# First weight slices split and summed by quarters, input loaded in four pieces, constants on ScalarE's queue, loads in order of use

## The reference

```
mod = silu(c) @ ada_w + ada_b;  shift, scale, gate = split(mod, 3)
h = rmsnorm(x, g_pre) * (1 + scale) + shift
z = h @ w_in
gates = sigmoid(h @ w_merge + b_merge)
...
out = rmsnorm((g_a * ya + g_b * yb) @ w_out, g_post)
y = x + gate * out
```

## Time and profile before

| what | us |
|---|---|
| median of 3 runs | 933.63 (932.96 to 933.76) |
| profiled execution, its own time | 933.39 |
| span of that execution | 931.6 |
| TensorE matmul busy | 905.5 (97%) |
| VectorE busy | 556.0 (60%) |
| ScalarE busy | 418.0 (45%) |
| GpSimd busy | 54.9 (6%) |
| DMA | mean 252 GB/s, 419 to 421 GB/s in the first 116 us |

### The profile page before, as it was taken

The page is one execution under the profiler, slowest core; times in us unless marked ns, Lnnn a source line. Parts: engine busy times, 40 slices in busy tenths (PEclk is TensorE's granted clock), DMA queues, the critical chain, the costliest instruction groups (busy, mean ns, idle before and its releaser), DMA issues.

```text
span 931.6 us, 18640 instructions
## 1 busy us (share of the span) xinstructions
PE 905.5 (97%) x7762; PEld 868.6 (93%) x7762; DVE 556.0 (60%) x808; ACT 418.0 (45%) x514; POOL 54.9 (6%) x38
## 2 busy tenths in 40 slices
PE   3899999999999999999999999999999999999997
PEld 1788989999999999999999999999999999999997
DVE  4777776476675767757576655336454444445554
ACT  4323227455565565646554434444344333343330
POOL 0000000001101010110102122000000000000000
PEclk9899999999999999999999999999999999999999
DMA  9999975848585684857675565476687666645535
GB/s 373 418 421 419 419 311 171 332 158 284 183 323 197 226 301 158 314 179 293 231 268 187 199 203 183 154 271 189 254 323 281 257 243 255 246 161 181 182 136 186
DMA packets 43322, 234.57 MB, mean 252 GB/s; under 512 B 9088, under 2 KB 14592, under 8 KB 16256
## 3 DMA queue, kind: packets, MB, share of 16 engines
q1 hardware_dynamic: 43264, 233.72, 68.0%
HBM read 219.33 MB, written 14.38 MB: 251 GB/s over the span
## 4 chain that ended last, share of the span: by engine, by line
PE 94%; DVE 2%; DMA 2%; issue 1%; POOL 1%; ACT 0%; SPq 0%; DVEq 0%; POOLq 0%; ACTq 0%
PE bank L429 25%; PE bank L430 24%; PE bank L431 24%; PE bank L481 4%; PE bank L482 3%; PE bank L483 3%; PE bank L403 3%; PE bank L413 1%; DMA raw<-stream 1%; PE bank L577 1%; PE bank L622 1%; PE bank L561 1%; DMA sel<-sel_in 1%; DVE raw L1429 1%; DVE w_lo L1028 0%
## 5 line engine op out<-in xcount | busy, mean ns | idle before, releaser
L429 PE MATMUL bank<-h_hi,w_hi 128*128 128x264 f32 x1280 | 368.2, 288 | 2.2 <-DVE w_lo L1028 1.3
L430 PE MATMUL bank<-h_lo,w_hi 128*128 128x264 f32 x1280 | 362.9, 283 | 0.0
L431 PE MATMUL bank<-h_hi,w_lo 128*128 128x264 f32 x1280 | 362.5, 283 | 0.0
L1028 DVE TENSOR_TENSOR w_lo<-raw,w_hi 128x2048 fp32r<-128x2048 f32 x119 | 272.3, 2288 | 142.1 <-PE bank L431 142.0
L712 ACT ACTIVATE w_hi<-raw 128x2048 fp32r<-128x2048 f32 x120 | 229.7, 1914 | 44.0 <-DMA raw<-stream 23.8
L429 PEld LDWEIGHTS bank<-h_hi,w_hi 128*128 128x128 f32 x1280 | 241.1, 188 | 8.5 <-issue 6.4
L430 PEld LDWEIGHTS bank<-h_lo,w_hi 128*128 128x128 f32 x1280 | 241.3, 189 | 0.3
L431 PEld LDWEIGHTS bank<-h_hi,w_lo 128*128 128x128 f32 x1280 | 240.1, 188 | 0.0
L481 PE MATMUL bank<-h_hi,w_hi 128*128 128x264 f32 x256 | 76.1, 297 | 4.5 <-DVE h_lo L1110 4.5
L482 PE MATMUL bank<-h_lo,w_hi 128*128 128x264 f32 x256 | 73.7, 288 | 0.0
L483 PE MATMUL bank<-h_hi,w_lo 128*128 128x264 f32 x256 | 73.6, 288 | 0.0
(11 more groups left out here) (180 smaller groups left out, 1181.4 us busy)
## 6 DMA issues: line engine op xcount, KB each, us to landing
raw<-stream SPq DMA_DIRECT2D x120, 1024.0 KB, 5.0
ada_ring<-ada SPq DMA_DIRECT2D x32, 1024.0 KB, 15.5
raw<-first_w SPq DMA_DIRECT2D x16, 1024.0 KB, 13.1
gate_ring<-ada SPq DMA_DIRECT2D x16, 1024.0 KB, 6.6
s_t<-sret SPq DMA_DIRECT2D x8, 1024.0 KB, 5.0
v_all<-v_dram SPq DMA_DIRECT2D x8, 1024.0 KB, 7.4
nret_s<-s_t SPq DMA_DIRECT2D x8, 1024.0 KB, 8.1
x_t<-xT SPq DMA_DIRECT2D x1, 2112.0 KB, 7.7
```

What stands on the lines that cost most here:

```text
L429: pe.matmul(out, wh[:, cols], hi[:, k, :], start=(k == 0), stop=False)
L430: pe.matmul(out, wh[:, cols], lo[:, k, :], start=False, stop=False)
L431: mm = pe.matmul(out, wl[:, cols], hi[:, k, :], start=False, stop=(k == depth - 1))
L1028: dve.tensor_tensor(lo, raw[:, c % 3, :], hi.bitcast(f32), ALU.subtract).then_inc(lo_ready, 1)
```

## The change

The core of the diff:

```
+BY_QUARTER, HIGH_BY_QUARTER = 5, 2
...
-            sp.dma_start(x_t[:, :, :], xT).then_inc(x_in, 16)
-            sp.dma_start(c_in[:, :, :], cT).then_inc(const_in, 16)
...
-            for p in range(8):
-                if p == 0:
-                    load_ada(p, range(4))
-                    load_slice(0)
-                else:
-                    load_ada(p, (0, 1))
-                    load_slice(2 * p)
-                    load_ada(p, (2, 3))
-                load_slice(2 * p + 1)
+            for n in range(4):
+                sp.dma_start(x_t[:, 4 * n:4 * n + 4, :], xT[:, 4 * n:4 * n + 4, :]).then_inc(x_in[n], 16)
+            load_ada(0, range(4))
+            load_slice(0)
+            for p in range(1, 8):
+                load_ada(p, (0, 1))
+                load_slice(2 * p - 1)
+                load_ada(p, (2, 3))
+                load_slice(2 * p)
+            load_slice(15)
...
-                if q - 1 in COND_VISITS:
-                    v = COND_VISITS.index(q - 1) + 1
-                    if v < 8:
-                        load_cond(v)
+                for s in range(2):
+                    if q - 1 - s in COND_VISITS[:7]:
+                        load_cond(COND_VISITS.index(q - 1 - s) + 1, s)
...
-                    if u == 2:
+                    if u == 1:
                         pe.wait_ge(x_sum, KT // 2)
...
+            def quarter(j, n):
+                if n == 0:
+                    pe.wait_ge(h_lo_ready, j // 2 + 1)
+                if n < 3:
+                    pe.wait_ge(lo_quarter, 3 * j + n + 1)
+                else:
+                    pe.wait_ge(lo_ready, j + 1)
+                for u in (2 * n, 2 * n + 1):
+                    if u < OWN_IN[j % 2]:
+                        own(j, u)
+                    else:
+                        pass_through(j, u - OWN_IN[j % 2])
...
             ada_phase(0)
             select(0)
+            for n in range(4):
+                quarter(0, n)
+            ada_phase(1, (0, 1))
+            quarter(1, 0)
+            ada_phase(1, (2, 3))
+            quarter(1, 1)
+            select(1)
+            quarter(1, 2)
+            quarter(1, 3)
+            for p in range(1, 7):
+                if 2 * p < BY_QUARTER:
+                    for n in range(4):
+                        quarter(2 * p, n)
+                else:
+                    even_slice(2 * p)
                 ada_phase(p + 1)
+                if 2 * p + 1 < BY_QUARTER:
+                    quarter(2 * p + 1, 0)
+                    select(p + 1)
+                    for n in range(1, 4):
+                        quarter(2 * p + 1, n)
+                else:
+                    odd_slice(2 * p + 1, between=p + 1)
```

```
+                normalize(p)
+                take_sum(2 * p - 1, 0)
+                make_h(p)
+                take_sum(2 * p - 1, 1)
+                split_slice(2 * p, 0)
+                take_sum(2 * p - 1, 2)
+                low_h(p)
+                take_sum(2 * p - 1, 3)
+                split_slice(2 * p, 1)
...
+            for b in range(3):
+                take_sum(14, b)
             split_slice(15, 0)
-            take_sum(14, 0)
             split_slice(15, 1)
-            take_sum(14, 1)
-            take_sum(14, 2)
+            take_sum(14, 3)
             split_slice(15, 2)
-            take_sum(14, 3)
+            take_sum(14, 4)
             split_slice(15, 3)
-            take_sum(14, 4)
-            take_sum(15, 0)
-            split(0, 0, parts=(0,))
...
+            for n in range(4):
+                take_sum(15, n)
+                split(0, 0, parts=(n,))
             take_sum(15, 4)
-            split(0, 0, parts=(2, 3))
             take_sum(15, 5)
```

More of the change, by code:

```diff
@@ L190, in build @@
         const_in = sem("const_in")
-        x_in = sem("x_in")
+        x_in = [sem(f"x_in{n}") for n in range(4)]
+        hi_quarter, lo_quarter = sem("hi_quarter"), sem("lo_quarter")
         trig_in = sem("trig_in")
@@ L463, in _, with ada_phase @@
             pe.wait_ge(const_ready, 1)
-            def ada_phase(p):
-                if p >= 1:
+            def ada_phase(p, slots=range(4)):
+                if p >= 1 and 0 in slots:
                     pe.wait_ge(mod_ready, p)
-                for s in range(4):
+                for s in slots:
                     u = 4 * p + s
-                    if u == 2:
+                    if u == 1:
                         pe.wait_ge(x_sum, KT // 2)
@@ L495, in pass_through @@
                 n = through(j, b)
-                if b == 0:
+                if b == 0 and j >= BY_QUARTER:
                     pe.wait_ge(lo_ready, j + 1)
@@ L525, in _ @@
             select(0)
-            for p in range(7):
-                even_slice(2 * p)
-                ada_phase(p + 1)
-                odd_slice(2 * p + 1, between=p + 1)
+            for n in range(4):
[13 more added lines that the diff above has]
+                    even_slice(2 * p)
+                ada_phase(p + 1)
+                if 2 * p + 1 < BY_QUARTER:
[5 more added lines that the diff above has]
+                    odd_slice(2 * p + 1, between=p + 1)
             even_slice(14)
@@ L719, in split_slice, with split_quarter @@
                 act.activation(w_hi[:, slot, :], raw[:, slot, :], ACT.Copy).then_inc(hi_ready, 1)
+            def split_quarter(j, n):
+                slot, cols = (j + 2) % 3, slice(512 * n, 512 * n + 512)
+                if n == 0:
+                    act.wait_ge(raw_loaded[slot], 16)
+                high = act.activation(w_hi[:, slot, cols], raw[:, slot, cols], ACT.Copy)
+                if n < 3:
+                    high.then_inc(hi_quarter, 1)
+                else:
+                    high.then_inc(hi_ready, 1)
+            act.dma_start(c_in[:, :, :], cT).then_inc(const_in, 16)
+            act.dma_start(vecs[:, :], vec).then_inc(const_in, 16)
+            act.dma_start(ident[:, :], ident_in).then_inc(const_in, 16)
+            act.dma_start(sel[:, :], sel_in).then_inc(const_in, 16)
             act.wait_ge(const_in, 64)
@@ L755, in _ @@
             ada_copy(0)
-            split_slice(0)
+            split_quarter(0, 0)
             split_h(0)
-            split_slice(1)
-            for p in range(1, 8):
+            for n in range(1, 4):
+                split_quarter(0, n)
+            for n in range(4):
+                split_quarter(1, n)
+            for p in range(1, 3):
+                ada_copy(p)
+                split_slice(2 * p)
+                split_h(p)
+                split_slice(2 * p + 1)
+            for p in range(3, 8):
                 split_slice(2 * p)
@@ L1114, in _ @@
             make_h(0)
+            split_slice(0, 0)
+            low_h(0)
+            for n in range(1, 4):
+                split_slice(0, n)
             for n in range(4):
[L1116 to L1118 removed]
+                take_sum(0, n)
+                split_slice(1, n)
+            take_sum(0, 4)
+            for p in range(1, 3):
+                if p == 2:
+                    for b in range(3):
+                        take_sum(2, b)
+                    split_slice(3, 0)
+                    split_slice(3, 1)
+                    take_sum(2, 3)
+                    split_slice(3, 2)
+                    take_sum(2, 4)
+                    split_slice(3, 3)
+                normalize(p)
[7 more added lines that the diff above has]
+                split_slice(2 * p, 1)
+                take_sum(2 * p - 1, 4)
+                take_sum(2 * p - 1, 5)
+                split_slice(2 * p, 2)
+                split_slice(2 * p, 3)
+            for p in range(3, 8):
+                for b in range(3):
+                    take_sum(2 * p - 2, b)
                 split_slice(2 * p - 1, 0)
[L1120 removed]
                 split_slice(2 * p - 1, 1)
[L1122 to L1123 removed]
+                take_sum(2 * p - 2, 3)
                 split_slice(2 * p - 1, 2)
[L1125 removed]
+                take_sum(2 * p - 2, 4)
                 split_slice(2 * p - 1, 3)
[L1127 removed]
                 normalize(p)
```

42 lines of the change are left out of this document (17 added, 25 removed).

## The result

The changed kernel takes **936.53 us** (median of 14 runs, 934.54 to 937.35), beside 933.50 for the kernel before on the same chip (14 runs). The ratio is 1.0029, with a 95% interval from 1.0022 to 1.0037: slower by 3.0 us. The forecast was 933.2, in a range of 930.1 to 935.3. The profiled execution took 936.81 us with a span of 935.0, against 931.6 before, so the trace shows 3.4 us to account for. The ratio is taken over all runs and not from the medians; by it the change is 2.7 us slower. The 14 runs spread over 2.8 us, and the spread goes with TensorE's mean granted clock: the three runs at 0.998 took 934.8 to 935.5 us, the three at 0.994 took 937.1 to 937.2.

A forecast was written before the change was run, and what follows sets the result against it. TensorE was taken as the bound, busy 638.6 of 640 us in the middle. Terms -2.3 + 0 + 0.3 + 1.6 + 1.2 + 1.4 - 0.9 - 1.3 gave 0.0; with 0.4 us for the clock, 933.63 became 933.2, range 930.1 to 935.3.

The forecast's parts named there:

- step 1: Loads at the start: constants on ScalarE's queue bring no byte sooner; squares end near 12.5 us instead of 16.7.
- Rival D: Start: constants land no sooner than 9.3 us, squares end at 16.7, ada units at 23.5; 935.2 us, chance 0.05.
- Steps 2 and 3: End of ada 0 to first product with h: product at 24.9 instead of 27.18 us, gain 2.3 together.
- Step 6: Slices' landing in the first stage: slices 2 and 4, loaded later, still land in time; no cost.
- Step 4: TensorE's low clock behind the first product: no gain, no loss; bounds 2.1 gained, 2.3 lost; 0.4 us gain added in the sum.
- Rivals B and C: TensorE's early clock: B, it does not fall, 931.5 to 931.9, chance 0.05; C, low longer or again, 937.2, chance 0.10.
- Step 5: Sums in slices 0 to 3: TensorE waits for VectorE, losing 0.3 in slice 0, 1.6 in slice 1, 1.2 in slice 3.
- Rival A: Early slices: VectorE has the sums out in time, so the 3.1 us loss falls away; 930.1 us, chance 0.15.
- Step 7: Slice 15: its last w_lo quarter stands behind the last sum of slice 14, loss 1.4 us.
- step 8: First stream tile: TensorE's 0.91 us wait for the last quarters of w_lo goes, gain 0.9.
- step 9: Merge stage: one ada tile instead of two ahead, the tile lands 2.5 us sooner, the 1.29 us wait goes, gain 1.3.

The follow-up runs named there:

- e2: The kernel before with only its four constants' loads moved to ScalarE's queue, x still one load: 940.89 us against 933.11, ratio 1.0082.
- e11: The change with each constants' load on ScalarE's queue cut in two by columns, eight loads of 128 rows: 945.49 us against 933.29 before, ratio 1.0137.
- e1: The change with the constants' loads back on SyncE's queue, behind the first quarter of x: 934.04 us against 933.11 before, ratio 1.0010.
- e12: The change with the constants' wait, cpad and the one_plus addition moved behind the squares of x: 934.13 us against 933.29 before, ratio 1.0010.
- e6: The kernel before with only the change's order of loads: 934.62 us against 933.37, ratio 1.0011.
- e7: The change with constants on SyncE's queue, and loads and orders from slice 1 on as before: 931.65 us against 933.37 before, ratio 0.9984.
- e3: The change with SyncE's order of loads and all written-out orders from slice 1 on as before: 932.07 us against 933.11 before, ratio 0.9986.
- e4: The change with VectorE's order around slice 15 as before: 935.01 us against 933.11 before, ratio 1.0015.
- e13: The kernel before with first stream tile split between slice 15's sums and gate pairs' loads one stream tile apart: 930.70 us against 933.24, ratio 0.9973.
- e5: The kernel before with only the two loads of each gate pair issued one stream tile apart: 932.21 us against 933.37, ratio 0.9988.

## Why the prediction was wrong, and where it was right

**The step that failed is step 1**: "The squares of x can start sooner: eight pairs at about 0.8 us each from 5.5 us on would end near 12.5." They began at 11.14, because the constants came at 10.7 and the squares are queued behind their wait. The pace of 0.8 us was right (11.14 to 17.2 for eight). What was not asked is when four small loads land on a queue of their own while the other queue is full. The trace of before had no such load, and the step took the absence of a row for "no cost". It should have been bounded by the nearest row, which was the pace of a tile, 2.5 us per load; e2's loads came at 2.6 to 2.7 behind x, the last at 17.0. Of the signs that the prediction named, D's came: the squares ended at 17.2 and not by 13.5. The step also named the Trainium skill's rule that issuing engines share the same DMA engines and drew from it only that no byte comes sooner; the turns that the queues take, packet by packet (e11), are what bears on it.

**Rival D** named this very place and chain: squares late, L471 before the second ada unit, units behind it until 23.5. The chain was right; its price was short by 1.3 us of the measured time (935.2 against 936.53), since it took 9.3 us as the latest landing where it was 10.7, and let part of the delay be absorbed. Its chance of 0.05 was small for the only rival with no row against it.

**Steps 2 and 3.** With the constants on time the first product came at 25.15 (e1) and 24.52 (e12), around the 24.9 forecast. The chain was right, but to book it as a gain was a second error, which shows only once the first is out of the way. Step 6 counted slices 2 and 4 and found them in time. It didn't count slice 1, which was moved 5 us later, past two ada tiles, and whose first quarter stands ahead of a sum of slice 0: 0.60 us in e1, 1.26 in e12, 1.41 in e6. And where slice 1 is not moved (e7), the ada tiles of phase 1 take the 2.3 us back. Step 6 also has two slips that cost nothing: slice 2 was the eighth tile behind the first ada tile, and in the change it landed at 37.9, not 36.5, still in time.

**Step 4**, the clock: bounds of -2.1 and +2.3, and 0.4 of gain taken; it cost 0.4. The low stretch moved with the start. Rivals B and C did not occur.

**Step 5** was right: 1.6 and 1.2 against 1.91 and 1.26, though the waits themselves are smaller (0.88 and 0.46) than the 1.2 and 0.8 foretold; the rest is spread over later units and the moved ada work, and the trace of the change does not split it further. Slice 0 was forecast at 0.3; without the clock's share it cost 0.5. Rival A is refuted by e3.

**Step 7** was right (1.12 us of wait, 1.1 to 1.5 by e4, 1.4 forecast), and so were **step 8** (0.9 forecast; 1.4 to 1.5 as e13 less e5 in the medians, but 1.1 in their traces, whose first products of the stream are at 153.30 and 154.43) and **step 9** (1.3; 1.2 in e5, 1.4 in the change). That product stands at 159.49 in the change and not within 1 us of 154.44, since the delay of the start is still in it.

Together: 3.04 us of the miss is the first product, 1.0 slice 0 with its clock, and the other steps come out 0.26 under their sum. That is the 3.8 us between the forecast's -0.4 and the trace's +3.4.

## What to carry to other kernels

In these kernels a small load that work waits for belonged on the queue of the big loads, right behind the first one it must not pass, not on an idle second queue: there it advanced by turns with the other queue, one packet for one, so that a small load took as long as a big one with the same number of rows. Look also at what stands behind a wait in program order without needing it; moving the wait (e12) was worth as much as moving the loads. And before an earlier start is booked as a gain, look at the next loads in order: where the DMA was full, the time came back as a wait for the next tile (e7), while the small gaps late in the kernel (steps 8 and 9) were kept in full (e5, e13).

## What the runs showed of the hardware

Four loads of 9 to 72 KB, issued within 1.4 us on ScalarE's queue, landed 1.7 to 2.1 us apart while x in quarters and then the first ada tile went through the other queue, and 2.6 to 2.7 us apart beside 1024 KB tiles, although the same four on SyncE's queue were all there by 6.4 us (e1). Their bytes didn't matter. What mattered was their packets, one per row and 16 per load, which went one for one with those of the other queue (329 and 329 from 12 to 18 us in e11). The clock's low stretch did not have one length: 26.5 to 33.4 us in the change, but 25.1 to 28.5 in e1, as its windows give it (0.78 over 24 to 26 is 0.9 us at half, 0.87 over 28 to 30 is 0.5):

```profile
24.00:26.00 2.00, 0.85 (x4) 0.78 1.03 426
26.00:28.00 2.00, 2.00 (x11) 0.50 1.02 426
28.00:30.00 2.00, 2.00 (x16) 0.87 1.03 422
```

What made it shorter there was not tested. It differs between runs of one kernel too, if the granted clock of the 14 runs of the change (0.994 to 0.998) is a measure of it. Of products 5.4 us lay under it in the change and 3.4 in e1; the 2.0 between them are worth 0.9 us, as much as some of the steps here.
